# Moving weight splits and the gain product around the first expert selection in a two-block transformer kernel

## The reference

```python
def block(xb):                                             # 128 tokens
    q = (xb @ wq).reshape(t, 8, 2, 128)                    # queries: 8 heads, 2 halves
    s = einsum('thpd,hpkd->thpk', q, subkeys)              # scores against 128 keys a half
    s_top, i_top = lax.top_k(s, 16)
    cand = (s_top[:, :, 0, :, None] + s_top[:, :, 1, None, :]).reshape(t, 8, 256)
    c_top, c_idx = lax.top_k(cand, 16)
    e = i1 * 128 + i2                                      # i1, i2: the chosen keys
    g = softmax(c_top)
    ue, ve = u[e], v[e]                                    # rows of 1024 floats each
    act = gelu(einsum('thkd,td->thk', ue, xb))
    return einsum('thk,thkd->td', g * act, ve)
```

## Time and profile before

| | us |
|---|---|
| median of three runs | 2023.56 |
| the three runs | 2023.01, 2025.4, 2023.56 |
| the profiled execution | 2023.01 |
| its span in the trace | 2021.2 |

### The profile page before, as it was taken

One profiled execution on the slowest core, in us unless ns is written; L12 is line 12 of the kernel. 1 busy time (PEld: TensorE's weight loads), 2 busy tenths in 40 slices (PEclk: granted clock), 3 DMA queues, 4 the chain that ended last, 5 costly groups with the idle time before them and its releaser, 6 DMA issues.

```text
span 2021.2 us, 22626 instructions
## 1 busy us (share of the span) xinstructions
PE 1702.1 (84%) x7622; PEld 1046.5 (52%) x7622; DVE 1339.4 (66%) x2922; ACT 914.3 (45%) x2366; POOL 841.9 (42%) x762
## 2 busy tenths in 40 slices
PE   8987988877778787889799989988899777778777
PEld 7985444422322222579799989983444222222222
DVE  4667776766776664499646774457776677667644
ACT  5554545444544443445324344464444444444443
POOL 4335333333333333367525465553333333333331
PEclk9999999999999999989899999999999999999999
DMA  7447999999999999544213333469999999999996
GB/s 253 131 164 283 421 421 422 421 421 422 421 422 421 421 421 422 202 132 126 71 56 96 104 106 124 157 216 421 421 421 421 421 421 422 421 422 421 421 422 286
DMA packets 102052, 637.60 MB, mean 315 GB/s; under 512 B 11264, under 2 KB 12544, under 8 KB 36144
## 3 DMA queue, kind: packets, MB, share of 16 engines
q0 software_dynamic: 75216, 543.73, 64.8%
q1 hardware_dynamic: 26720, 92.43, 14.1%
HBM read 635.07 MB, written 1.05 MB: 315 GB/s over the span
## 4 chain that ended last, share of the span: by engine, by line
PE 38%; DMA 35%; DVE 16%; ACT 8%; issue 3%; POOL 0%; SPq 0%; DVEq 0%; ACTq 0%
DMA arena<-in_uv,arena 32%; PE pb L604 18%; PE pb L357 4%; PE pb L359 4%; PE pb L358 4%; ACT arena L1053 3%; DMA spare<-in_uv,arena 3%; DVE arena L1630 3%; PE pb L430 1%; PE pb L741 1%; PE pb L732 1%; ACT parts L903 1%; DVE arena L1821 1%; DVE parts L1283 1%; ACT arena L1048 1%
## 5 line engine op out<-in xcount | busy, mean ns | idle before, releaser
L604 PE MATMUL pb<-arena 128*128 128x512 f32 x1848 | 912.6, 624 | 220.5 <-ACT arena L1053 219.1
L1630 DVE SCALAR_TENSOR_TENSOR arena<-arena,pb 128x1024 f32<-128x1024 f32 x462 | 563.3, 1219 | 372.5 <-DMA arena<-in_uv,arena 372.5
L2156 POOL DMA_INDIRECT arena<-in_uv,arena x462 | 439.0, 950 | 721.8 <-PE pb L604 682.8
L604 PEld LDWEIGHTS pb<-arena 128*128 128x128 f32 x1848 | 323.1, 192 | 776.9 <-ACT arena L1053 518.0
L2134 POOL TENSOR_TENSOR parts<-ring,parts 128x512 fp32r<-128x512 f32 x228 | 341.5, 1517 | 341.0 <-ACT parts L903 338.8
L1045 ACT ACTIVATE arena<-arena 128x1 f32<-128x1 f32 x512 | 103.3, 202 | 625.1 <-DVE arena L1630 571.0
L903 ACT ACTIVATE parts<-ring 128x512 fp32r<-128x512 f32 x328 | 198.1, 626 | 199.3 <-PE pb L359 189.9
L1053 ACT ACTIVATE arena<-cst,arena 128x128 f32<-128x128 f32 x512 | 205.5, 401 | 48.3 <-PE pb L604 1.1
L357 PE MATMUL pb<-xl,parts 128*128 128x256 f32 x704 | 220.9, 314 | 4.3 <-DVE xl L1315 2.5
L358 PE MATMUL pb<-xh,parts 128*128 128x256 f32 x704 | 200.7, 285 | 0.0
L359 PE MATMUL pb<-xh,parts 128*128 128x256 f32 x704 | 200.6, 285 | 0.0
(11 more groups left out here) (297 smaller groups left out, 1776.6 us busy)
## 6 DMA issues: line engine op xcount, KB each, us to landing
ring<-in_w_in SPq DMA_DIRECT2D x108, 512.0 KB, 3.6
ring<-in_wq SPq DMA_DIRECT2D x32, 512.0 KB, 5.9
ring<-in_w_out SPq DMA_DIRECT2D x16, 512.0 KB, 3.6
arena<-in_uv,arena POOLq DMA_INDIRECT x462, 20.2
ring<-in_wa SPq DMA_DIRECT2D x8, 512.0 KB, 3.6
ring<-in_wb SPq DMA_DIRECT2D x8, 512.0 KB, 3.8
arena<-in_sk POOLq DMA_DIRECT2D x2, 1024.0 KB, 7.9
arena<-in_tail POOLq DMA_DIRECT2D x1, 1280.0 KB, 11.2
```

The source lines that it names most:

```text
L604: ins = pe.matmul(ys[hf][:, :], diags[:, k % 4, :], lands[k % LANDS][:, D + hf * 512:D + (hf + 1) * 512], start=k % (8 * K) == 0, stop=k % ...
L1630: ve.scalar_tensor_tensor(z, z, 1.0, xg[t], ALU.mult, ALU.mult, accum_out=hidden[:, k:k + 1]).then_inc(*up("v_dot", ("dot", e, k)))
L2156: gp.indirect_dma_start(lands[k % LANDS], None, rows_uv, bass.IndirectOffsetOnAxis(ap=eidx[:, k:k + 1], axis=0)).then_inc(*up(f"dma_rows{k ...
```

## The change

In both blocks the change does three things. VectorE splits wq 12 and wq 13 and computes `with_gain(0)` ahead of `chosen(0)` rather than behind it. The other four splits (wq 14 to 17) stay behind `gates(0)`. GpSimd splits wq 4 and wq 5 ahead of the three DMAs at L2146 to L2149 rather than behind them. The arguments of `ahead` sum up to what they were, so no instruction is added or dropped.

```diff
@@ vector_program, experts()
                 row_scale(tag)
                 vq.wait_ge(*on((tag, "rs")))
-                ahead(12 - PARTS)
+                ahead(8)
+                with_gain(0)
                 for _ in chosen(0):
                     pass
-                with_gain(0)
                 gates(0)
-                ahead(PARTS)
+                ahead(4)
@@ gpsimd_program, ahead of experts(1, ...)
-            ahead(18 * 4 - PARTS + 4)
+            ahead(18 * 4)
@@ gpsimd_program, experts(), behind the three DMAs
-                ahead(PARTS - 4 + 8)
+                ahead(8)
                 ahead(8 * 4 - PARTS - 8)
@@ gpsimd_program, ahead of experts(2, ...)
-            ahead(8 * 4 - PARTS + 4)
+            ahead(8 * 4)
             experts(2, "w_out2", d["sk2"], d["ffn2"], d["fin2"], d["uv2"])
```

## The result

The changed kernel took 2038.34 us (median of 4 runs, 2035.16 to 2040.49) against 2023.94 us (4 runs), a ratio of 1.0069 with a 95% interval of 1.0052 to 1.0087. That is +14.4 us. The forecast was 2039.9 us, from +16.4. The profiled execution took 2036.71 us, with a span of 2034.9 us, 13.7 us more than before.

What follows compares the result with a forecast made beforehand. The DMA transfers were taken to bound the gather loops, so a late first gather delays everything behind. 7.6 + 1.6 - 1.2 = 8.0 and 8.0 + 1.6 - 1.2 = 8.4 us, together 16.4, gave 2039.9 us; range 2032 to 2049.

Steps and rivals of the forecast that it cites:

- chosen(0) waits for wq 13's high part: VectorE ahead of chosen(0): the split waits for ScalarE's high part, so chosen(0) starts 7.6 and 8.0 us later.
- keyed(0) waits for the keys: TensorE's keyed(0): keys issued 12.05 us later in the first block, landing in 6.6 us; 1.6 us stall in each block.
- clock falls in that gap (rival): TensorE's gap between item(0) and keyed(0): a lower clock costs 2 us more per block; booked at nothing, 30%.
- the selection itself: chosen(0), from its start to the first gather's issue: no change of its length was booked.
- the loop: Transfer-bound gather loops: a late start is not given back; only slab 10 loaded earlier saves 1.2 us a block.
- rival 2: TensorE's clock falls before keyed(0): 2043.9 us, with slower key landings of 7.6 and 8.2 us up to 2046.5; 30%.
- The early slab: wq's slab 10 loads ahead of the first gather, taking 0.52 MB out of the full stage: 1.2 us saved per block.
- What comes back: Between the indices and dot(0): 2.7 us of VectorE work disappears, but the gather lands no earlier; booked at nothing.

Runs made afterwards that it cites:

- e4: VectorE's part of the change alone (wq 12 and 13 split and with_gain(0) ahead of chosen(0)), against the kernel before: ratio 1.0046, +9.3 us.
- e1: Kernel before with VectorE splitting wq 12 and 13 ahead of chosen(0), with_gain(0) left behind it: ratio 1.0039, +7.9 us.
- e2: Kernel before with only with_gain(0) moved ahead of chosen(0): ratio 1.0001.
- e3: Kernel before with GpSimd's part of the change alone (wq 4 and 5 split ahead of the three DMAs): ratio 1.0015, +3.0 us.
- e10: The changed kernel run again, unaltered, against the kernel before: ratio 1.0072, +14.6 us.
- e5: Kernel before with with_gain(0) computed nine times ahead of chosen(0) as a pause on VectorE, splits and DMAs unmoved: ratio 1.0126, +25.5 us.
- e7: Kernel before with wq 12 and 13 split by GpSimd, behind wq 11, so slab 10 loads ahead of the first gather: ratio 0.9985, -3.0 us.
- e8: Kernel before with the edits of e6 and e7 together (GpSimd splits wq 10 to 13 once chosen(0) is past L1572): ratio 1.0000.
- e9: Kernel before with the edit of e6 and with_gain(0) ahead of chosen(0): ratio 0.9980, -4.1 us, median 2021.22 us.
- e6: Kernel before with GpSimd's splits of wq 10 and 11 held until chosen(0) is past L1572: ratio 0.9988, -2.4 us.

## Why the prediction was right, and where its terms were off

The time, 2038.34 us, lies 1.6 us below the forecast and inside its range. Taken apart by the two profiled executions, against the steps of the prediction:

| step | forecast, both blocks | measured |
|---|---|---|
| chosen(0) waits for wq 13's high part | +7.6, +8.0 | +7.5, +7.8 (e4) |
| keyed(0) waits for the keys | +1.6, +1.6 | +1.2, +1.4 |
| clock falls in that gap (rival) | 0, 0 | 0, +1.6 |
| the selection itself | 0, 0 | -1.0, -1.1 |
| the loop | -1.2, -1.2 | -1.5, -1.7 |
| sum | +8.0, +8.4 | +6.2, +7.9 |

The sums are made before rounding. The measured sum is 14.1 us; the spans differ by 13.7, because the changed execution entered the first block's edge 2.0 us late and lost 2.4 us less than that of before in the second block's mixer, where the change does nothing. Single executions of one kernel differ by that much (2022.0 to 2028.3 us in 21 runs of the kernel before), so the parts are compared from one event to the next and not by absolute times. That forecast and measurement lie so close is in part luck: the clock's +1.6 us, booked at nothing, stands against -2.1 us in the selection and -0.8 us in the loop that were not booked either.

**The wait for wq 13** was read right, with its place, its releaser and its size (unrounded, the prediction's terms give 7.5 and 7.9 us): 10.01 instead of 2.55 us behind keyed(0) in e4, and 10.00 instead of 2.17. e1 shows that its split alone is 6.1 and 6.5 of it, and e4 against e1 that with_gain(0), which filled idle time in e2, adds its 1.3 us once it stands behind the wait. The same instruction is free in one place of the stream and not in the other.

**The keys.** The mechanism was right and its size a little too large: they landed 6.2 and 6.4 us after their issue, not 6.6. e3 shows this part alone, with 6.3 us twice. The slow landing that the prediction kept with rival 2 is possible at the new place too: 7.92 us once, in the second block of e10.

**The clock** was left at nothing and given 30%, as a thing of both blocks. It fell in one: behind 1.96 us of idle in the first block it stayed at 2.4 GHz, and behind 2.13 us in the second it fell to 1.2 GHz, with the start of chosen(0) 11.58 us behind keyed(0) where e4, without the gap, has 10.00. e3 and e10 fall in the second block too and not in the first. The length of the gap alone doesn't decide it: 1.96, 2.03 and 2.06 us left the clock where it was, 2.05, 2.13 and 3.69 us were followed by the lower level, and in all six TensorE had been busy without a break for 3.1 us before. Three executions are too few to say what does.

**The loop.** That it gives nothing back was the base of the sum, and e5 shows it for 13 us a block. The early slab was booked at 1.2 us in each block; e1 shows 0.9, e7 1.4 and 1.1, e8 1.5 and 1.4. The step that was off is "What comes back": "I book nothing here" for the work that disappears from between the indices and dot(0). For the first dot product it holds, and more than that: in each of the kernels with with_gain(0) ahead of chosen(0) (changed, e2, e4, e5, e9, e10) that product starts 7.1 to 7.8 us behind the issue of its gather, in all others 5.7 to 6.1. But a first gather that lands later didn't make the loop longer. Behind with_gain(0) stood the splits of wq 14 to 17, and behind these the loads of slabs. e2 moves with_gain(0) alone, and its loads of slabs 10 to 12 are issued from 1.33 us after the first gather on, where it was 2.66 us before (174.96 - 173.63 against 173.50 - 170.84), at a time when the DMA engines are not yet full; its loop is 0.4 and 0.5 us shorter. Against the kernel with the same other edits e4's loops are 0.4 and 0.8 us shorter (than e1's) and e9's 0.4 and 0.3 us (than e6's), but e5, with the same early loads, has -0.5 and +0.5 us. So a small gain is likely, its cause was not tested by itself, and single executions can't size it.

**What was missed** is the -1.0 and -1.1 us in the selection. The prediction took the length of chosen(0) as fixed. The trace of before had the sign of it in one instruction that took 1.42 us where its like takes 0.41. e6 removes the overlap and with it the long instruction, e8 moves the overlap and the long instructions move along, and e5 shows the same from the other side, with splits on GpSimd that grew from 7.7 to 10.3 us. The Trainium skill, page "SBUF — State Buffer", section "🔬 SBUF: two separate sides", has the rule: GpSimd shares one pair of ports with VectorE; a VectorE instruction contends for it when it runs in a 2-port mode, which casts and operations with a scalar can do, or when it reads two inputs from SBUF while GpSimd's instruction reads SBUF too, and whichever instruction starts first keeps it to its end while the other waits. The traces agree, with 1.42 and 0.41 us for L1569, which has two inputs. L1572, L1584, L1589 and L1591 were held up too, and they have one tensor input each; they are such casts and operations with a scalar, but whether they ran in a 2-port mode no run here shows. The searches for maxima ran beside the same splits undisturbed (0.43 us for L1574 in e6 and in the changed kernel alike).

## What to carry to other kernels

In an in-order stream the cost of moving an instruction is the cost of its wait, paid by all that stands behind it: two splits of 1.3 us together, moved ahead of a selection that starts a transfer-bound loop, made it start 6.1 and 6.5 us later, since one of them had to wait; with_gain(0), 1.3 us too, delayed nothing where the engine was idle anyway, and 1.3 us behind that wait. Look for the last thing that releases a saturated stage and put nothing ahead of it that waits for another engine; loads that such a stage would carry can be had before it by an engine that is idle there. And before a serial chain's length is taken as fixed, compare each of its instructions with its like elsewhere in the trace.

## What the runs showed of the hardware that I had not expected

- A small VectorE instruction beside a split on GpSimd of 1.3 us lasted up to 1.27 us instead of 0.17 (L1589 of e8, 128x16 values). Instructions of 128x16, 128x32 and 128x256 values lost about the same in the worst case, 1.0 to 1.1 us: what is lost went with what was left of the split and not with their own size. Each instruction of chosen(0) that was held up, in all the kernels, ended 0.03 to 0.04 us behind the end of a split that had started before it, L1569 0.28 us behind.
- Both sides pay: in e5 six of the 18 instructions of L1622 in each block took 1.64 to 1.79 us beside GpSimd's splits and the others 0.75 to 0.76, and the splits beside them took 1.72 to 1.81 us (one 1.53) instead of 1.25 to 1.30.
- TensorE's clock fell behind an idle of 2.13, 2.05 and 3.69 us in the second block of the changed kernel, of e3 and of e10, and not behind 1.96, 2.03 and 2.06 us in the first. TensorE had been busy without a break for 3.1 us before each of these gaps, behind an idle of 0.6 us.
- The same DMA of the keys, issued with the same other loads around it, landed after 6.2 to 6.4 us in five of six cases and after 7.9 us in the sixth (the second block of e10).
